# Moving work between the steps of a one-core hybrid decoder layer: gate steps, adaLN units, norm sums, attention steps and an early reload

## The chip, the cores and the metric

The kernel runs on one core of a Trainium2 chip, in float32 throughout. The metric is the device time of one execution in microseconds (us). The kernel before was timed three times: 1274.6, 1275.09 and 1276.74 us, median 1275.09.

## The reference

One decoder layer is run for a prompt of 512 tokens and for 8 sample tokens, with shared weights and D = 1024. `c` gives six adaLN vectors, which scale, shift and gate:

```python
shift1, scale1, gate1, shift2, scale2, gate2 = split(silu(c) @ w_ada + b_ada, 6)
h = modulate(rmsnorm(x, norm1_g), shift1, scale1)
gq, gk, gv, gr, glr, aq, ak, av, ga, gb = split(h @ w_in)
logg = log_sigmoid(glr @ gla_wg2 + gla_bg) / 16          # forget gates of branch A
y_a  = (rmsnorm(gla(gq, gk, gv, logg)) * silu(gr)) @ w_branch_a
# branch B: 3 groups of 8 heads, (window, dilation) = (128,1), (512,4), (2048,16);
# the groups' outputs are joined with weights from their softmax denominators
y_b  = o_att @ w_branch_b
x = x + gate1 * ((sigmoid(ga) * y_a + sigmoid(gb) * y_b) @ w_out)
h2 = modulate(rmsnorm(x, norm2_g), shift2, scale2)
a, b = split(h2 @ w_up)
x = x + gate2 * ((silu(causal_conv3(a)) * b) @ w_down)
y = rmsnorm(x, normf_g)
```

The samples attend to cached keys and values, and all the updated states and caches are outputs too.

## The kernel before

Activations lie feature-major: 8 tiles of 128 features by 520 tokens (512 of the prompt, 8 samples). Each weight matrix is streamed by SyncE in units of at most 1 MB into two slots `wraw`. Float32 precision is made out of three passes: ScalarE rounds a unit to `whi` (`split_hi`, L349), VectorE takes the rest as `wlo` (`split_lo`, L362), and TensorE multiplies hi by hi, hi by lo and lo by hi (`three_pass`, L378). A unit of two output tiles is 96 matmuls of 260 columns. This stream fills nearly the whole execution; everything else is pushed in between its matmuls.

How it is pushed in: the other work of a phase is written as generators (one each for TensorE, ScalarE and VectorE) that `yield` after each step. `Between` counts places in the stream (with `fine=True` eight places a unit, one after each 12 matmuls, without it four) and at each place advances the generator by as many steps as keep the steps spread evenly over the places. Where there are more steps than places, some places get two steps with no stream matmul between them. All three engines count alike, and semaphores order what they exchange. An engine executes its instructions strictly in the written order, so a step that waits stops the stream behind it.

The places and names that matter here:

- `gla_in_*`: the 28 steps beside the seven units of the phase `gla_in`. Steps 0 to 3 make the forget gates of the prompt: one matmul (L924), on ScalarE Abs, Exp and Ln (L887 to L889) with a load of another function table ahead of Exp and of Ln, and on VectorE one operation (L974). Step 4 does it for the samples, step 5 prepares the relative bias (L985), 6 to 9 are its matmuls (L939, L945).
- `heads_tok_*`, `attend_*`, `sample_*`, `join_*`: the steps of an attention phase. Values, keys and the new rows are turned to token-major, then come 8 or 16 score steps (scores L1543, exp L1678, turned probabilities L1555, times values L1568), then the cached keys of the samples. The last phase (`att2`) goes on with `join_*`: the joined output is turned (L1829) and split (`b2H`, `b2L`), then the samples' softmax (L1835, L1897 to L1910, L1841), their cached values (L1854) and their output (L1861, L1863). The stream of `att2` is the four units `gb`, whose tiles ScalarE copies (L433) and SyncE stores to a scratch tensor `raw_gates` (L446). The block of `att2` ends when SyncE has seen all these stores land (L1948).
- Each block ends in a barrier of all engines. The next block multiplies by w_branch_b (`bb`, two units of four tiles), w_branch_a (`ba`) and w_out (`wo`), four units of two tiles each. POOL reloads the raw gates `raw4` and the stored GLA output `oT4` (2 MB) at the start of this block; ScalarE takes sigmoids (L2020), VectorE multiplies (L2119, L2122), ScalarE rounds the product (L2067) and copies the `bb` tiles (L2078).
- adaLN: w_ada is cut in 24 units of 256 columns. A unit is 16 matmul records (L528), a copy (L547), a turn (L539) and an addition into `mod` (L552). Units 8 to 19 are interleaved with the stream; units 20 to 23 (all of them `gate2`, first read in the down projection) come in a row behind the last `wo` unit.
- Beside them runs the norm ahead of the FFN: squares on ScalarE (L602), their sum over the 8 tiles on VectorE (L611), a matmul with ones (`sums_pe`, L563), mean, root and Newton step (L570 to L597), a broadcast by matmul (L589). In the next block `modulate_ffn_*` makes `actH` and `actL` tile by tile, and the first FFN unit follows it tile by tile.

Of the kernel before, what the change touches and what calls it, by code (L numbers as in the profile page):

```python
# [5 lines left out]
F32 = mybir.dt.float32  # L6
# [5 lines left out]
P = 128  # L12
D = 1024
KD = D // P
TP = 512
# [20 lines left out]
N_HEAD, N_TAIL, N_ADA = 8, 20, 24  # L36
# [104 lines left out]
def program(nc, w, o, con):  # L141
# [23 lines left out]
    with ctx:  # L165
# [392 lines left out]
        def sums_pe(pe, i, bank, t):  # L558

            pe.wait_ge(s("sq_added"), (KD - 1) * i)  # L560
            for n in range(5):
                m = P if n < 4 else NS
                last = pe.matmul(ps[0:m, bank, n:n + 1], t[:, P * n:P * n + m], ones[:, 0:1], start=True, stop=True)  # L563
            last.then_inc(s("sq_summed"), 1)
# [34 lines left out]
        def square_act(act, i, k, X, tmp):  # L599
            if k >= 2:  # L600
                act.wait_ge(s("sq_added"), (KD - 1) * (i - 1) + max(1, k - 2))
            act.activation(tmp["sq"][:, k % 2, :], X[:, k, :], ACT.Square).then_inc(s("sq_ready"), 1)  # L602

        def square_dve(dve, i, k, tmp):
# [4 lines left out]
            if k >= 2:  # L609
                dve.wait_ge(s("sq_added"), (KD - 1) * (i - 1) + k - 1)  # L610
            dve.tensor_tensor(tmp["t"], tmp["sq"][:, 0, :] if k == 1 else tmp["t"], tmp["sq"][:, k % 2, :], ALU.add)\  # L611
               .then_inc(s("sq_added"), 1)

        def modulate_ffn_dve(dve, X, tmp):

            g = vec[:, V_N2:V_N2 + KD].unsqueeze(2).to_broadcast([P, KD, NC])
            shift, scale = 3 * KD, 4 * KD
            dch.link(dve, dve.scalar_tensor_tensor(tmp["A"], mod[:, scale:scale + KD, :], 1.0, g, ALU.add, ALU.mult))  # L618
            hs = tmp["hs"]
            dve.wait_ge(s("r_spread"), 2)  # L620
            dch.link(dve, dve.tensor_tensor(hs, X[:, :, TP:T], rS.unsqueeze(1).to_broadcast([P, KD, NS]), ALU.mult))
            dch.link(dve, dve.tensor_tensor(hs, hs, tmp["A"][:, :, 1:NC], ALU.mult))  # L622
            dve.tensor_tensor(hs, hs, mod[:, shift:shift + KD, 1:NC], ALU.add).then_inc(s("h_ready"), 1)

            def low(k):
                dve.wait_ge(s("h_hi"), KD + 2 + k)
                dve.scalar_tensor_tensor(actL[:, k, 0:TP], tmp["hf"][:, k % 2, 0:TP], mod[:, shift + k, 0:1],  # L627
                                         actH[:, k, 0:TP].bitcast(F32), ALU.add, ALU.subtract).then_inc(s("h_split"), 1)

            for k in range(KD):  # L630
# [4 lines left out]
                if k == 0:  # L635
                    dve.wait_ge(s("h_hi"), KD + 1)
                    dve.tensor_tensor(actL[:, :, TP:T], hs, actH[:, :, TP:T].bitcast(F32), ALU.subtract)
                else:
                    low(k - 1)
            low(KD - 1)  # L640

        def modulate_ffn_act(act, tmp):

            act.wait_ge(s("h_ready"), KD + 1)
            act.activation(actH[:, :, TP:T], tmp["hs"], ACT.Copy).then_inc(s("h_hi"), 1)
            for k in range(KD):
                act.wait_ge(s("h_normed"), KD + k + 1)
                act.activation(actH[:, k, 0:TP], tmp["hf"][:, k % 2, 0:TP], ACT.Identity, bias=mod[:, 3 * KD + k, 0:1])\
                   .then_inc(s("h_hi"), 1)

# [243 lines left out]
        V_LAG = 15  # L894
        IN_STEPS = 4 * len(GLA_IN)
# [20 lines left out]
        def gla_in_pe(pe):  # L916
            for p in range(IN_STEPS):
# [3 lines left out]
                if p < 4:  # L921
                    if p >= 2:
                        pe.wait_ge(s("g_ready"), p - 1)
                    pe.matmul(ps[:, 4 + p % 2, :], lrT[0:GR + 1, P * p:P * p + P], wg2, start=True, stop=True)\  # L924
                      .then_inc(s("z_ready"), 1)
                elif p == 4:
# [5 lines left out]
                elif 6 <= p < 6 + NG:  # L932
                    g = p - 6
# [7 lines left out]
                elif p == 6 + NG:  # L941
# [11 lines left out]
        def gla_in_act(act):  # L953
            for p in range(IN_STEPS):
                if p < 4:
                    act.wait_ge(s("z_ready"), p + 1)
                    if p >= 1:
                        act.wait_ge(s("g_ready"), p)
# [512 lines left out]
        def heads_tok_act(act, g):  # L1471
# [4 lines left out]
            for c in KOUT[g]:  # L1476
                yield
# [1090 lines left out]
```

## Time and profile before

| | |
|---|---|
| median of three runs | 1275.09 us |
| the profiled execution: time | 1278.76 us |
| its span, first to last instruction | 1277.1 us |
| TensorE matmul busy | 1204.9 us (94%) |
| VectorE, ScalarE, GpSimd busy | 623.9, 453.6, 107.2 us |
| mean granted TensorE clock | 0.968 of full |
| DMA | 229.41 MB, mean 180 GB/s |
| a weight split of 2048 columns, mean: ScalarE (L2260), VectorE (L2316) | 1.9, 2.3 us |
| a w_in load of 1 MB, issue to landing, median (38 issues) | 5.3 us |
| a w_ada load of 1 MB into `arena`, the same (12 issues) | 12.0 us |
| TensorE's waits for copies of turned probabilities (L1688) | 3.0 us in five, longest 1.1 |

TensorE is the busy engine. A busy time is not all useful time: where the granted clock is 0.50 (1.2 GHz in place of 2.4 GHz), a matmul is busy for longer. "Idle before" in a row is the time in which that engine did nothing ahead of that instruction, with the engine or transfer that ended the wait. The views used below are the waits (who waited for whom), windows (busy time and clock of given stretches), the timeline (instructions by time) and the chain of work that ended last.

### The profile page before, as it was taken

Reading aid. Unit: us, or ns where it says so; the run is one execution under the profiler, and the core shown is the slowest. Engines: PE = TensorE matmul, PEld = TensorE weight load, DVE = VectorE, ACT = ScalarE, POOL = GpSimd, SP = SyncE. Lnnn points to the kernel's source line nnn. Section 1 sums busy time; section 2 is a strip of 40 time slices with the busy share of each in tenths; the row PEclk is TensorE's granted clock in tenths of the full one; section 3 lists DMA queues with packets and bytes.
Section 4 is the critical chain, followed back from the end, with each engine's and each line's share of the span. In section 5 each row is a group of like instructions: output and inputs, shape, how many; then the busy total and the mean of one; then the engine's idle time right before and its main releaser. Section 6 shows DMA issues by size and latency. Waiting matters only on the chain. (4 is left out here: it accounts for less than half of the span.)

```text
span 1277.1 us, 23207 instructions
## 1 busy us (share of the span) xinstructions
PE 1204.9 (94%) x9743; PEld 1139.8 (89%) x9743; DVE 623.9 (49%) x1003; ACT 453.6 (36%) x652; POOL 107.2 (8%) x189
## 2 busy tenths in 40 slices
PE   5898999999989999999988989998999999999997
PEld 4777999988989999989887789987999999999997
DVE  3523224554534554266478175556666556643333
ACT  3273223544344441353243154224323332322222
POOL 0000002111011001110211111000000000000000
PEclk8898999999999999999988899997999999999999
DMA  9653539755345324333427477712878888256661
GB/s 303 182 186 118 170 117 346 274 181 169 104 149 163 100 64 161 114 104 104 130 71 260 151 247 280 235 34 67 264 256 279 285 265 258 83 176 222 222 224 67
DMA packets 166017, 229.41 MB, mean 180 GB/s; under 512 B 7644, under 2 KB 148342, under 8 KB 164636
## 3 DMA queue, kind: packets, MB, share of 16 engines
q1 hardware_dynamic: 148720, 123.72, 31.8%
q10 hardware_dynamic: 1684, 54.56, 11.7%
q0 software_dynamic: 15536, 50.01, 11.5%
q8 instruction: 59, 0.97, 0.3%
q14 instruction: 18, 0.15, 0.0%
HBM read 204.58 MB, written 81.87 MB: 224 GB/s over the span
## 5 line engine op out<-in xcount | busy, mean ns | idle before, releaser
L378 PE MATMUL ps<-actH,whi 128*128 128x260 f32 x2064 | 436.6, 293 | 10.7 <-DVE actL L627 4.0
L378 PE MATMUL ps<-actH,wlo 128*128 128x260 f32 x2064 | 419.9, 285 | 0.0
L378 PE MATMUL ps<-actL,whi 128*128 128x260 f32 x2064 | 419.2, 285 | 0.0
L378 PEld LDWEIGHTS ps<-actH,whi 128*128 128x128 f32 x2064 | 322.5, 192 | 29.9 <-issue 24.6
L378 PEld LDWEIGHTS ps<-actL,whi 128*128 128x128 f32 x2064 | 322.6, 191 | 0.0
L378 PEld LDWEIGHTS ps<-actH,wlo 128*128 128x128 f32 x2064 | 322.4, 191 | 0.0
L362 DVE TENSOR_TENSOR wlo<-wraw,whi 128x2048 fp32r<-128x2048 f32 (+2 forms) x95 | 141.2, 1498 | 155.1 <-ACT whi L349 154.8
L349 ACT ACTIVATE whi<-wraw 128x2048 fp32r<-128x2048 f32 (+2 forms) x95 | 119.4, 1274 | 122.4 <-PE ps L378 91.6
L433 ACT ACTIVATE arena<-ps 128x520 f32<-128x520 f32 x74 | 44.5, 601 | 221.3 <-PE ps L378 213.1
L378 PE MATMUL ps<-gH,whi 128*128 128x260 f32 x352 | 71.8, 285 | 0.0
L378 PE MATMUL ps<-gL,whi 128*128 128x260 f32 x352 | 71.3, 284 | 0.0
L378 PE MATMUL ps<-gH,wlo 128*128 128x260 f32 x352 | 71.2, 284 | 0.0
L2316 DVE TENSOR_TENSOR wlo<-wraw,whi 128x2048 fp32r<-128x2048 f32 x22 | 50.4, 2293 | 25.4 <-ACT whi L2260 25.4
L1678 ACT ACTIVATE arena<-arena 128x128 f32<-128x128 f32 (+1 forms) x96 | 34.1, 419 | 65.2 <-DVE arena L1651 65.1
L378 PEld LDWEIGHTS ps<-gL,whi 128*128 128x128 f32 x352 | 55.0, 190 | 0.0
L378 PEld LDWEIGHTS ps<-gH,whi 128*128 128x128 f32 x352 | 54.8, 190 | 0.1
L378 PEld LDWEIGHTS ps<-gH,wlo 128*128 128x128 f32 x352 | 54.7, 190 | 0.0
L2260 ACT ACTIVATE whi<-wraw 128x2048 fp32r<-128x2048 f32 x22 | 42.1, 1913 | 7.0 <-issue 7.0
L1646 DVE SCALAR_TENSOR_TENSOR arena<-ps,arena 128x512 f32<-128x512 f32 (+1 forms) x32 | 20.9, 654 | 35.9 <-PE ps L1543 35.2
L547 DVE COPY arena<-ps 128x256 f32<-128x256 f32 x24 | 10.1, 422 | 57.4 <-PE ps L528 57.4
L2242 POOL DMA_DIRECT2D out_conv_p<-arena x22 | 11.4, 518 | 316.6 <-DVE arena L2357 214.8
L2267 ACT ACTIVATE arena<-arena 128x520 f32<-128x520 f32 x22 | 14.1, 640 | 64.4 <-DVE arena L2333 64.4
(338 smaller groups left out, 1420.0 us busy)
## 6 DMA issues: line engine op xcount, KB each, us to landing
wraw<-in_w_in SPq DMA_DIRECT2D x38, 1024.0 KB, 5.3
out_win_s<-in_cache_win ACTq DMA_DIRECT2D x16, 2046.0 KB
wraw<-in_w_up SPq DMA_DIRECT2D x44, 512.0 KB, 5.8
out_win_s<-in_cache_win ACTq DMA_DIRECT2D x8, 2044.0 KB
arena<-in_w_ada SPq DMA_DIRECT2D x12, 1024.0 KB, 12.0
wraw<-in_w_ada SPq DMA_DIRECT2D x12, 1024.0 KB, 5.2
raw_gates<-arena SPq DMA_DIRECT2D x24, 260.0 KB, 6.2
arena<-raw_gates POOLq DMA_DIRECT2D x24, 260.0 KB, 4.3
```

The source lines that it names most:

```text
L349: ins = act.activation(whi[:, v % 2, c], wraw[:, u % 2, c], ACT.Copy)
L362: ins = dve.tensor_tensor(wlo[:, v % 2, c], wraw[:, u % 2, c], whi[:, v % 2, c].bitcast(F32), ALU.subtract)
L378: last = pe.matmul(ps[:, 2 * (n % 2) + a, 0:HT], wt, X[:, k0 + j, a * HT:a * HT + HT], start=begin and j == 0 and wt is hi and X is H, sto ...
L433: act.activation(halves(to), banks(n), ACT.Copy).then_inc(tile_read["act"], 1)
L547: dve.tensor_copy(rows[:, a % 2, :], ps[:, 7, 0:2 * P]).then_inc(ada_tok, 1)
L1646: dve.scalar_tensor_tensor(sv, ps[:, 4 + n % 2, 0:nh * J].rearrange("p (h k) -> p h k", k=J), SCALE, biasT[:, hs, lo:hi], ALU.mult, ALU.ad ...
L1678: last = act.activation(sv, sv, ACT.Exp, bias=own(g, c)[:, h:h + 1])
L2242: pool.dma_start(o["conv_p"][:, col], ast[0:2, store.slot, :]).then_inc(s(f"stored{store.slot}"), 16)
L2260: act.activation(whi[:, vn % 2, :], wraw[:, (up0 + 1 + d) % 2, :], ACT.Copy).then_inc(hi_ready, 1)
L2267: act.activation(sg5, acc, ACT.Sigmoid).then_inc(s("ffn_sig"), 1)
L2316: dve.tensor_tensor(wlo[:, vn % 2, :], wraw[:, (up0 + 1 + d) % 2, :], whi[:, vn % 2, :].bitcast(F32), ALU.subtract).then_inc(lo_ready, 1)
```

## The change

It edits the order of work and a few waits; almost no instruction is added or removed.

1. `gla_in`: the gate steps stand at every other step (0, 2, 4, 6), that of the samples at 8, the bias matmuls from 10 on; VectorE prepares the bias at step 7.
2. Last attention phase: the transposes of values and keys are taken in pairs, four steps in place of eight; one empty step ahead of the first score step and two behind it; the join gets two empty steps ahead of the turned softmax, the samples' cached values have six steps of their own, the output has one, and an empty step closes the phase: 39 steps in place of 36 over 32 places. In all attention phases the first scores wait for ScalarE's copies of the new rows only and no longer for VectorE's subtraction (L1503) behind them; the sample steps wait for that.
3. POOL issues the first four raw-gate loads and the load of `oT4` at the end of `att2`, not at the start of the next block. There the sigmoid of each `bb` unit's first tile stands ahead of the weight split.
4. N_TAIL goes from 20 to 22: units 20 and 21 are interleaved behind the third and fourth `ba` unit, and only 22 and 23 stand behind the last `wo` unit.
5. The ones matmul ahead of the FFN is in two parts, which add up in PSUM: the sum over seven tiles, and the eighth square by itself. VectorE's last addition goes. The FFN scale (L618) is computed ahead of the sums. Unit 23's turn is moved into the FFN block, and TensorE's root broadcast is behind the turn of unit 22.
6. `modulate_ffn_*`: the prompt's first tile comes ahead of the small operations on the samples.

```diff
-N_HEAD, N_TAIL, N_ADA = 8, 20, 24
+N_HEAD, N_TAIL, N_ADA = 8, 22, 24
...
-        def sums_pe(pe, i, bank, t):
-            pe.wait_ge(s("sq_added"), (KD - 1) * i)
+        def sums_pe(pe, bank, part, first):
             for n in range(5):
...
+                last = pe.matmul(ps[0:m, bank, n:n + 1], part[:, P * n:P * n + m], ones[:, 0:1], start=first and n == 0,
+                                 stop=not first and n == 4, skip_group_check=True)
+            return last
...
+            dve.wait_ge(s("r_spread"), 2)
+            normed(0)
+            dch.link(dve, dve.tensor_tensor(hs, X[:, :, TP:T], rS.unsqueeze(1).to_broadcast([P, KD, NS]), ALU.mult))
+            dch.link(dve, dve.tensor_tensor(hs, hs, tmp["A"][:, :, 1:NC], ALU.mult))
+            dve.tensor_tensor(hs, hs, mod[:, shift:shift + KD, 1:NC], ALU.add).then_inc(s("h_ready"), 1)
+            low(0)
...
+        Z_STEP, ZS_STEP, B_STEP = (0, 2, 4, 6), 8, 10
...
+        HSTEPS = (5, 8, 4)
+        GAPS = (0, 0, 1)
...
-            pe.wait_ge(s("new_tok"), token(g, 2))
+            pe.wait_ge(s("new_tok"), token(g, 1))
...
-        JOIN_STEPS = 4 + 2 + 1 + VSTEPS
+        JOIN_STEPS = 4 + 5 + VSTEPS + 2
...
                 for i in range(VSTEPS):
                     load_values(i)
+                pool.wait_ge(outs, n_outs[0])
+                pool.wait_ge(s("oj_T"), 4)
+                for r in range(4):
+                    slot_landed(pool, "vc", r, 16)
+                    load_raw(pool, r)
+                pool.wait_ge(s("spT"), 2)
+                pool.dma_start(oT4.rearrange("p k t -> p (k t)"), od).then_inc(s("o_back"), 16)
...
-                    split_hi(act, U[u]["i"] + 1)
                     for m in range(4):
                         q = 4 * j + m
                         sigmoid_act(act, q)
+                        if m == 0:
+                            split_hi(act, U[u]["i"] + 1)
...
                 ada_pe(pe, N_TAIL)
-                ada_turn_pe(pe, N_TAIL, ada4)
-                sums_pe(pe, 1, 5, n2["t"])
-                for a in range(N_TAIL + 1, N_ADA):
-                    ada_pe(pe, a)
-                    if a == N_TAIL + 2:
-                        spread_root_pe(pe, 1, tok2)
-                    ada_turn_pe(pe, a, ada4)
+                pe.wait_ge(s("sq_added"), KD - 2)
+                sums_pe(pe, 5, n2["t"], True)
+                pe.wait_ge(s("sq_ready"), KD)
+                sums_pe(pe, 5, n2["sq"][:, (KD - 1) % 2, :], False).then_inc(s("sq_summed"), 1)
+                ada_pe(pe, N_TAIL + 1)
+                ada_turn_pe(pe, N_TAIL, ada4)
+                spread_root_pe(pe, 1, tok2)
...
+                ada_turn_pe(pe, N_TAIL + 1, ada4)
                 first_unit()
```

What the change does to TensorE's order is seen at three places. First, the first scores of `att2` (L1543 before, L1586 now) and the turned probabilities (L1555, L1598); L378 is the stream. Before:

```order
L378 MATMUL ps<-actL,whi 128x260 x2
L378 MATMUL ps<-actH,wlo 128x260 x2
L1543 MATMUL ps<-arena 128x128 [waits s_read,new_tok]
L1543 MATMUL ps<-arena 128x128 x7
L1555 MATMUL ps<-cst,arena 128x128 [waits pT_ready,p_ready]
L1555 MATMUL ps<-cst,arena 128x128 x3
L378 MATMUL ps<-actH,whi 128x260 x2
```

and now:

```order
L378 MATMUL ps<-actL,whi 128x260 x2
L378 MATMUL ps<-actH,wlo 128x260 x2
L1586 MATMUL ps<-arena 128x128 [waits s_read,new_tok]
L1586 MATMUL ps<-arena 128x128 x7
L378 MATMUL ps<-actH,whi 128x260 x2
L378 MATMUL ps<-actL,whi 128x260 x2
L378 MATMUL ps<-actH,wlo 128x260 x2
```

The turned probabilities stood right behind the scores; now 36 stream matmuls (18 rows) are between them.

Second, the end of `att2`: the cached values (L1854 before), the samples' output (L1861 and L1863 before, L1916 and L1920 now) and the branch that ends the block (L1939, L2013). Before:

```order
L378 MATMUL ps<-actH,wlo 128x260 x2
L1854 MATMUL ps<-arena 32x512 [waits slot_in4]
L1854 MATMUL ps<-arena 32x512 x3
L1861 MATMUL ps<-cst,arena 128x8 [waits spT]
L1863 MATMUL ps<-arena 128x4 x2
L1861 MATMUL ps<-cst,arena 128x8
L1863 MATMUL ps<-arena 128x4 x2
L1861 MATMUL ps<-cst,arena 128x8
L1863 MATMUL ps<-arena 128x4 x2
L1861 MATMUL ps<-cst,arena 128x8
L1863 MATMUL ps<-arena 128x4 x2
L1939 UNCONDITIONAL_BRANCH
```

and now:

```order
L1916 MATMUL ps<-cst,arena 128x8 x3
L1920 MATMUL ps<-arena 128x4 [waits spT]
L1920 MATMUL ps<-arena 128x4 x3
L1920 MATMUL ps<-arena 128x4 [waits spT]
L1920 MATMUL ps<-arena 128x4 x3
L378 MATMUL ps<-actH,whi 128x260 x2
L378 MATMUL ps<-actL,whi 128x260 x2
L378 MATMUL ps<-actH,wlo 128x260 x2
L378 MATMUL ps<-actH,whi 128x260 x2
L378 MATMUL ps<-actL,whi 128x260 x2
L378 MATMUL ps<-actH,wlo 128x260 x2
L2013 UNCONDITIONAL_BRANCH
```

Before, the last stream matmuls stood ahead of the last four values and of the output; now 12 of them stand behind the output, and nothing is behind these.

Third, TensorE between the last `wo` unit and the FFN: adaLN units (L528), their turns (L539), the sums (L563 before, L562 now), the root broadcast (L589, L590). Before (the turn of unit 22, unit 23 and its turn follow the last row shown):

```order
L563 MATMUL ps<-cst,arena 128x1 [waits sq_added]
L563 MATMUL ps<-cst,arena 128x1 x3
L563 MATMUL ps<-cst,arena 8x1
L528 MATMUL ps<-arena,scP 32x256 [waits ada_tok,ada_tail_in]
L528 MATMUL ps<-arena,scP 32x256 x7
L539 MATMUL ps<-cst,arena 128x9 [waits ada_read,ada_tok]
L539 MATMUL ps<-cst,arena 128x9
L528 MATMUL ps<-arena,scP 32x256 [waits ada_tok,ada_tail_in]
L528 MATMUL ps<-arena,scP 32x256 x7
L589 MATMUL ps<-cst,arena 128x128 [waits r_ready]
L589 MATMUL ps<-cst,arena 128x128 x3
L590 MATMUL ps<-cst,arena 128x8
```

and now:

```order
L562 MATMUL ps<-cst,arena 8x1
L562 MATMUL ps<-cst,arena 128x1 [waits sq_ready]
L562 MATMUL ps<-cst,arena 128x1 x3
L562 MATMUL ps<-cst,arena 8x1
L528 MATMUL ps<-arena,scP 32x256 [waits ada_tok,ada_tail_in]
L528 MATMUL ps<-arena,scP 32x256 x7
L539 MATMUL ps<-cst,arena 128x9 [waits ada_read,ada_tok]
L539 MATMUL ps<-cst,arena 128x9
L589 MATMUL ps<-cst,arena 128x128 [waits r_ready]
L589 MATMUL ps<-cst,arena 128x128 x3
L590 MATMUL ps<-cst,arena 128x8
L2115 UNCONDITIONAL_BRANCH
```

Two adaLN units are gone from this place, a second set of sums is added, and the block ends right behind the broadcast.

## Rows read from the trace of the kernel before

**Rows 1.** Waits of TensorE, whole span: who was waited for: us, times, longest.
```profile
PE ps L1555 <- ACT arena L1678: 4.0, 2, 2.8
PE ps L378 <- ACT arena L2078: 4.0, 1, 4.0
...
PE ps L939 <- DVE arena L985: 3.3, 1, 3.3
PE ps L1841 <- DVE arena L1906: 3.1, 1, 3.1
...
PE ps L924 <- DVE arena L974: 2.1, 2, 1.1
...
PE ps L1543 <- DVE query_parts L1503: 1.7, 2, 1.5
...
PE ps L1835 <- DVE b2L L1891: 1.0, 1, 1.0
...
PE ps L378 <- PEq L1939: 0.9, 1, 0.9
PE ps L1861 <- DVE arena L1931: 0.9, 1, 0.9
```
**Rows 2.** Windows, TensorE: stretch, length, busy (instructions), granted clock, DMA share, GB/s.
```profile
100.20:107.00 6.80, 5.50 (x21) 0.50 0.49 154
639.50:646.20 6.70, 4.02 (x18) 0.50 0.84 256
694.10:700.80 6.70, 4.74 (x23) 0.50 0.21 81
718.00:728.10 10.10, 9.17 (x40) 0.50 0.36 110
738.50:741.70 3.20, 3.20 (x17) 0.50 0.56 133
858.00:878.30 20.30, 15.17 (x81) 0.50 0.19 53
```
**Rows 3.** Chain that ended last: start us, us, what; a unit at each clock.
```profile
872.38 14.40 PE ps L378 x96
...
1003.46 11.54 PE ps L378 x96
```
**Rows 4.** Timeline of ScalarE in gla_in: start us, us, instruction, idle before.
```profile
80.33 0.60 ACT L887 ACTIVATE arena<-ps 128x512 f32<-128x512 f32 x1 [0.33 <-DVE arena L974]
80.94 1.28 ACT L888 ACT_TABLE_LOAD   x1
...
85.63 0.60 ACT L887 ACTIVATE arena<-ps 128x512 f32<-128x512 f32 x1 [0.82 <-DVE arena L974]
```
**Rows 5.** SyncE's waits, 690 to 730 us.
```profile
SPq L1948 <- DMA raw_gates<-arena: 1.7, 1, 1.7
```
**Rows 6.** Timeline of ScalarE about the end of att2.
```profile
714.91 0.60 ACT L433 ACTIVATE arena<-ps 128x520 f32<-128x520 f32 x1 [9.91 <-PE ps L378]
```
**Rows 7.** Timeline of VectorE: the first product with the reloaded GLA output.
```profile
736.14 0.70 DVE L2122 TENSOR_TENSOR arena<-arena 128x520 f32<-128x520 f32 x1 [8.61 <-DMA arena<-gla_out]
```
**Rows 8.** Timeline of TensorE: an interleaved adaLN unit, then the end of wo.
```profile
755.35 1.07 PE L528 MATMUL ps<-wraw,scP 128*32 128x256 f32 x16
...
756.82 0.36 PE L378 MATMUL ps<-a2H,whi 128*128 128x260 f32 x1
...
852.91 1.07 PE L528 MATMUL ps<-arena,scP 128*32 128x256 f32 x16
...
855.90 1.15 PE L563 MATMUL ps<-cst,arena 128*128 128x1 f32 x9
...
861.35 2.08 PE L589 MATMUL ps<-cst,arena 128*128 128x128 f32 x8
```
**Rows 9.** Timeline of VectorE ahead of the first FFN unit.
```profile
868.90 0.06 DVE L2307 MEMSET arena<- 128x5 f32 x1 [0.35 <-PEq L2039]
...
869.30 0.22 DVE L621 TENSOR_TENSOR arena<-arena,ps 128x64 f32<-128x64 f32 x1
```

More of the change, by code:

```diff
@@ L1453, in heads_tok_pe @@
                 yield
-            for i, c in enumerate(KOUT[g]):
+            for i, c in enumerate(KOUT[g]) if g < NG - 1 else ():
                 if i >= 2:
@@ L1469, in heads_tok_pe @@
             yield
+            yield from pause(g, 1)
         def heads_tok_act(act, g):
@@ L1474, in heads_tok_act @@
                 act.activation(avt[:, c, :], ps[:, 4 + c % 2, :], ACT.Copy).then_inc(s("av_tok"), 1)
-                yield
-            for c in KOUT[g]:
+                if g < NG - 1 or c % 2:
+                    yield
+                if g == NG - 1 and c % 2:
+                    yield
+            for c in KOUT[g] if g < NG - 1 else ():
                 yield
@@ L1484, in heads_tok_act @@
             yield
+            yield from pause(g, 1)
         def heads_tok_dve(dve, g):
-            for c in range(4):
+            for c in range(4 if g < NG - 1 else 0):
                 yield
             for i in range(len(KOUT[g])):
+                if g == NG - 1 and i % 2 == 0:
+                    yield
                 n = K0[g] + i
@@ L1659, in attend_dve @@
                 yield
+                if j == 0:
+                    yield from pause(g, 2)
             settle(len(st))
@@ L1692, in attend_act @@
                 yield
+                if j == 0:
+                    yield from pause(g, 2)
             yield
@@ L1877, in join_act @@
             act.activation(SS, SS, ACT.Exp, bias=small[0:NR, 0:1], accum_out=small[0:NR, 1:2]).then_inc(s("sm_p"), 1)
-            for _ in range(2 + VSTEPS):
+            for _ in range(5 + VSTEPS):
                 yield
@@ L1937, in join_dve, with load_raw @@
             yield
+            yield
+        oT4 = at(0, KD, T)
+        ya, yb = at(12480, KD, T), at(16640, KD, T)
+        raw4 = at(20800, 4, T)
+        RAW = list(range(KD)) + [q + k * KD for q in range(KD) for k in (1, 2)]
+        def load_raw(pool, r):
+            q = RAW[r]
+            pool.dma_start(raw4[:, r % 4, :], rawd[:, T * q:T * q + T]).then_inc(slot_in("raw", r % 4), 16)
         with nc.Block() as block:
@@ L1995, in program @@
         G = {k: units(k) for k in ("bb", "ba", "wo", "up", "dn")}
-        RAW = list(range(KD)) + [q + k * KD for q in range(KD) for k in (1, 2)]
         def residual_dve(dve, n, q, gate):
```

199 lines of the change are left out of this document (112 added, 87 removed).

## The prediction

> **What bounds the kernel now.** I read the waits of TensorE first, then the granted clock in windows around each of them, then the timeline where an edit touches it. TensorE is busy for 94% of the span, and a unit of 96 stream matmuls takes 11.54 us at the upper clock [rows 3], so one place of 12 takes 1.44 us and one of 24 takes 2.9 us. The time is TensorE's: it moves only by what TensorE waits for, by the instructions it issues, and by the clock that it is granted. The reader is to see in [rows 1] that almost every wait ahead of the FFN is one that the change touches, and in [rows 2] that stretches at half the clock (1.2 GHz in place of 2.4) lie right behind such waits. A matmul there takes twice as long, so a low stretch costs half of its busy time. The FFN itself runs without gaps worth a term, and no edit reaches into it.
>
> **The sum is made against the profiled execution**, 1278.76 us (span 1277.1 and 1.7 around it). That is 3.7 above the median of the three runs, 1275.09; I take the same difference off the median.
>
> **Gate steps of gla_in.** One gate tile goes through ScalarE and VectorE in 5.3 us (85.63 less 80.33, [rows 4]), and ScalarE starts the next one only when VectorE is through. The steps stood one place of 2.9 us apart, so TensorE waited 2.1 us in two waits (L924), and 3.3 us for the bias (L939), which VectorE reached only behind the last gate [rows 1]. At every other place there are 5.8 us for 5.3, and more where an adaLN unit lies between; the bias is prepared at step 7 for a matmul at step 10. The steps also leave room on ScalarE for its two tile copies and one weight split per unit. Behind the 3.3 us wait the clock was at half over a stretch with 5.50 us busy [rows 2], 2.7 lost. The bounds are 5.4 (clock falls all the same) and 8.1; with the longest wait gone I take 8.1. **-8.1**
>
> A rule of the Trainium skill speaks against this. The row shows a table load of 1.28 us [rows 4], and the whole gate, with two of them, in 5.3. "ScalarE: Activation LUTs", section "What ACT_TABLE_LOAD costs", adds some 1.38 us of drain to a load, 2.7 us for each switch. If two drains had still to be added, an estimate by that page is 8.1 us a gate, over the 5.8, and TensorE would go on waiting; the trace does not agree, as 5.3 holds everything.
>
> **The first scores of all attention phases** waited for VectorE's subtraction, 1.7 us in two waits, the longer of 1.5 in the last phase [rows 1]. The other 0.2 goes, because the copies on ScalarE are done earlier. **-0.2**
>
> **Scores of the last phase.** Of the 1.5 us about 0.7 goes, one VectorE operation of such a width [rows 7], and 0.8 for ScalarE's three copies stays. The turned probabilities stood right behind the scores and waited 2.8 us for ScalarE's exponentials (the longer of the two under L1678, [rows 1]). Now three places, 4.3 us of stream, lie between: gone. The half clock behind it had 4.02 us busy [rows 2], 2.0 lost. The pairs of transposes ahead cost nothing: the instructions are the same, and each wait on a copy has at least one place in between. The key copy waits for the store of the buffer two copies earlier, and the pairs leave that store as much time as before. The short waits for copied probabilities further on (3.0 us in five over the whole span, by the table) stay, since those steps keep their distance. -0.7 -2.8 -2.0 = **-5.5** (bounds 3.5 and 6.3).
>
> **Join.** Before, 1.0 us for the last split and 3.1 us for the samples' softmax [rows 1]. The two empty steps put two places, 2.9 us, over the softmax: 0.2 remains. But the pair of joined tiles turned at one place shortens the cover of the splits, so the 1.0 stays, and VectorE now has a piece of the weight split ahead of the softmax and one behind it, on which the last unit's first matmul waits: I take 1.3 for both together. New waits 2.5 in place of 4.1: -1.6 (bounds 0 and -4.1). The half clock with 4.74 us busy goes, as no wait of 3 us is left: -2.4. **-4.0**
>
> **End of that phase.** The wait for the picked values, 0.9 (L1861), goes: 12 matmuls cover it. But the same step list now ends with stream matmuls. Before, the last values and the output stood behind the last stream tile, some 7 us in which ScalarE copied that tile (714.91, 0.60 long, [rows 6]) and SyncE stored it and saw it land 1.7 us after its issue [rows 5]; the gap at the block's end was 0.9 [rows 1]. Now nothing covers that: 0.7 for the copy and its start, about 2.0 for issue and landing, 0.5 for the barrier (the gap of 0.9 without the two small operations in it), 3.2 us. That is +2.3. The output's matmuls of 4 and 8 columns hardly load TensorE; before, the clock was at half from their middle on, up to 5.4 us into the next block (the fourth stretch of [rows 2]). I expect the same now, with the last 12 matmuls in it, 1.44 us more. -0.9 +2.3 +1.4 = **+2.8** (bounds -3.2 to +5).
>
> **Start of the bb units.** ScalarE could not copy the second tile before it had rounded a product that waited for `oT4`: VectorE was idle for 8.6 us until 736.14 [rows 7], and TensorE waited 4.0 us (L2078, [rows 1]). Issued from the step of the softmax on, some ten places earlier, it lands before the block begins; POOL has nothing else queued there, and what it waits for (old stores, the turned join, the weighted new values) lies behind it by then. Per tile ScalarE has three operations of 0.6 us [rows 6] in 2.9, and the split behind the first sigmoid still ends a tile early. The half clock behind the wait, 3.20 busy, goes too: 1.6. **-5.6** (bounds 4.0 and 5.6)
>
> **Between wo and the FFN.** The last stream matmul ends at 852.9, the first of the FFN starts at 872.38 [rows 3, 8]. In between now: unit 22, then the sum over seven tiles, which VectorE ends one addition and TensorE one turn earlier, at about 855.0 in place of 855.90 [rows 8]; two sets of sums for one, 2.3 us for 1.15, to 857.2, about where they ended before. The mean, root and Newton step run beside unit 23 (1.07) and a turn, to 859.4 with the lower clock setting in at 858. The broadcast, 2.6 us at that clock with its sample part (2.08 of it in the row), ends at 862.0 instead of 863.9, and the block ends there, without two units and three turns at half clock. VectorE starts the next block 0.6 us later, at 862.6 in place of 868.90 [rows 9]. From there to the first FFN matmul it took 3.5 us; the scale and three small operations, 0.22 us long [rows 9] and about 0.25 each with the step to the next, are no longer ahead: 2.5, so 865.1. That is -7.3. The first unit took 14.40 us in place of 11.54 because of the clock [rows 3]; I leave it so, and TensorE at half clock is slower than the tiles come. Units 20 and 21 reappear in the stream, each 1.47 us with its turn (756.82 less 755.35, [rows 8]) at the upper clock: +2.9. If the last weights arrive in time, no wait is added there. **-4.4** (bounds -2.5 and -7)
>
> **Sum:** -8.1 -0.2 -5.5 -4.0 +2.8 -5.6 -4.4 = -25.0. Profiled 1278.8 - 25.0 = 1253.8, and for the median 1275.1 - 25.0 = **1250.1 us**.
>
> **Rivals.**
> - *The waits go and the clock does not come back.* The four low stretches that I count as gone cost 2.7, 2.0, 2.4 and 1.6, 8.7 in all; if shorter waits close by keep them, -16.3 is left: 1258.8 us. For it: the clock also fell at 718 behind a wait of only 0.9 with matmuls of few columns. Against it: waits of 1.1 (L924, L1688) left it up.
> - *The clock stays up at the end of the last phase.* The 12 full matmuls behind the output could hold it: 1.4 is not paid and the half of 9.17 us [rows 2], 4.6, is gained: 1244.1. Against it stands the new idle of 3.2 us right behind them.
> - *A late weight load.* The load of the second wo unit has to wait until unit 21 is used, which is the start of the first wo unit. It has 11.5 us less the two splits of the table (1.9 and 2.3), 7.3 us. The table gives 5.3 us as median for a weight load, but 12.0 for loads that start among many; the tail loads start at the same time. With 12.0 TensorE waits 4.7: 1254.8.
> - *The gates still stall* (the change would not do what it says). If ScalarE is held up in each gate by two more operations of a table load's length [rows 4], 2.6 us, three steps lack 2.1 each, 6.3 in all: 1256.4. No row supports it. The page named above would make it so.
> - *Slower than before.* The last store, on which the block's end now hangs bare. It landed 2 us after issue when nothing else was in flight; now POOL puts four reloads and 2 MB into the DMA engines in that phase. The 2 MB took 12 us from the block's start to 736; a store held up as long costs 10, and 1260 results. It turns the sum over only if the store takes 25 us more, for which the rows have no example.
>
> **Chances.** Forecast 0.60, clock does not come back 0.13, clock stays up 0.13, late load 0.06, gates 0.03, held store up to 1270 0.02, slower than before 0.03. The forecast's own range is 1246 to 1254, from the bounds of the join (2.5), the block's end (2.5) and the tail (2). The range for 8 in 10 takes in most of the first two rivals: 1243.5 to 1259. A measurement of this kernel tells 0.2%, 2.6 us, from no change; all cases but the last two are faster by more. Faster 0.95, same 0.02, slower 0.03.
>
> **What would show it.** In the profile after: no wait above 0.5 us under the gate and bias matmuls and no 0.50 clock about 100 us; none between the first scores and the turned probabilities; the softmax wait under 1 us; a gap of about 3 us at the end of the last attention phase, ended by the landing of a store to raw_gates; none for the bb tiles; 12 us in place of 19.5 between the last wo and the first FFN matmul. I am wrong if a gap of 2 us or more stands anywhere else, if the low stretches stay in number, or if the gap at the block's end is as short as before.

## The result, and the profile after

| | before | changed kernel |
|---|---|---|
| time, median | 1274.84 us (1273.21 to 1276.74, 4 runs) | 1259.67 us (1257.51 to 1262.34, 4 runs) |
| ratio | | 0.9881, 95% interval 0.9858 to 0.9905 |
| profiled execution: time, span | 1278.76, 1277.1 us | 1262.34, 1260.7 us |
| mean granted clock | 0.968 | 0.973 |

The kernel is 15.2 us faster (12.1 to 18.1 by the interval). The forecast was 25.0 us, and its range ended at 1259.0, just below the median.

The waits of TensorE in the profile after (line waited at, who was waited for: us in all, times, longest) answer to [rows 1]:

```profile
PE ps L1885 <- DVE b2L L1950: 7.2, 1, 7.2
...
PE ps L378 <- PEq L2013: 3.4, 1, 3.4
...
PE ps L1586 <- ACT arena L1521: 0.7, 1, 0.7
...
PE ps L1879 <- DVE b2L L1950: 0.7, 1, 0.7
```

Three things are to be seen. The waits under the gates (L924, L939), under the softmax (L1841, now L1893) and at the second bb tile (L378 for ScalarE) have no row any more; of the two on the exponentials (L1555, now L1598) the one of 2.8 is gone. The gap at the block's end is 3.4 in place of 0.9, as forecast. And one long wait is new, the longest of the span: 7.2 us under the transposes of the joined tiles (`join_pe`), for VectorE's `b2L`. No term had it. Two small ones are new as well, 1.0 us ahead of the sums (L562) and 0.5 us ahead of unit 23's turn (L539), between wo and the FFN, where the forecast added none.

The windows (stretch, length, busy us of TensorE, weight load, VectorE, ScalarE and GpSimd, granted clock, DMA share, GB/s) of the low stretches answer to [rows 2]:

```profile
281.60:285.00 3.40, 3.40 (x20) 2.59 (x21) 0.00 (x0) 1.31 (x4) 2.04 (x3) 0.51 1.03 362
677.70:687.80 10.10, 5.12 (x23) 4.68 (x24) 6.19 (x14) 3.17 (x5) 0.00 (x0) 0.50 0.20 70
708.40:721.90 13.50, 10.14 (x47) 9.87 (x46) 3.89 (x4) 4.94 (x6) 0.54 (x1) 0.50 0.36 130
848.40:861.90 13.50, 11.44 (x58) 10.09 (x50) 9.35 (x25) 3.95 (x8) 0.00 (x0) 0.50 0.28 80
```

Those at 100, 639, 694 and 738 us are gone. The one at 677.7 is new, right behind the 7.2 us wait, and costs half of its 5.12 busy, 2.6 us. The one at 281.6 is new too (3.40 busy, up to 1.7 lost); it lies in the GLA phase, which no edit touches.

"Half of the busy time", in the prediction and here, is a little too much for the stream. TensorE's timeline where the clock comes back (start, us, instruction), pairs of stream matmuls at 0.50 and then at full clock:

```profile
717.35 0.64 PE L378 MATMUL ps<-b2H,whi 128*128 128x260 f32 x2
717.78 0.64 PE L378 MATMUL ps<-b2L,whi 128*128 128x260 f32 x2
...
722.05 0.40 PE L378 MATMUL ps<-b2H,wlo 128*128 128x260 f32 x2
722.29 0.40 PE L378 MATMUL ps<-b2H,whi 128*128 128x260 f32 x2
```

A pair follows the last by 0.43 us at half clock and by 0.24 at full, 1.8 times and not twice, so that a low stretch full of them costs 44% of its busy time.

Followed back, the 7.2 us lead through three engines. ScalarE's timeline (start, us, instruction, idle before and what ended it):

```profile
662.39 0.60 ACT L433 ACTIVATE arena<-ps 128x520 f32<-128x520 f32 x1 [3.26 <-PE ps L378]
...
669.08 2.00 ACT L1931 ACTIVATE b2H<-ps 128x512 fp32r<-128x512 f32 x2 [4.52 <-PE ps L1879]
670.85 0.66 ACT L349 ACTIVATE whi<-wraw 128x512 fp32r<-128x512 f32 x1
678.21 0.60 ACT L433 ACTIVATE arena<-ps 128x520 f32<-128x520 f32 x1 [6.70 <-DMA raw_gates<-arena]
678.71 1.96 ACT L1931 ACTIVATE b2H<-ps 128x512 fp32r<-128x512 f32 x2
```

TensorE waits for `b2L`, VectorE for `b2H` (L1931), and ScalarE's `b2H` stands behind its copy of the fifth gb tile (L433). That copy waited 6.70 us for a store: the spill buffer has two halves, and the store of the third gb tile still read this one. The queues of SyncE and of GpSimd show why (issue, us, operation):

```profile
662.67 0.38 SPq L335 DMA_DIRECT2D wraw<-in_w_branch_b  x1
663.10 0.98 SPq L446 DMA_DIRECT2D raw_gates<-arena  x2
```

```profile
653.92 3.03 POOL L2035 DMA_DIRECT2D arena<-in_cache_win  x4 [24.97 <-DVE arena L1691]
656.94 2.40 POOL L2038 DMA_DIRECT2D arena<-in_cache_win  x4
```

The second pair of rows is the loads of cached values. The third tile was copied at 647.65 (0.60 long), but its store was issued at 663.10 only: in `stream_sp` it stands behind the next weight load, which waits for a weight slot. By then the loads of cached values (5.1 MB: four of 1024 KB, four of 256 KB) had been under way for 9 us. DMA issues of 662.3 to 664.5 us (x, KB each, median us to landing):

```profile
wraw<-in_w_branch_b SPq DMA_DIRECT2D x1, 1024.0 KB, 14.9
raw_gates<-arena SPq DMA_DIRECT2D x2, 260.0 KB, 15.1
```

The same two rows before, where the store was issued at 668.45 and the value loads at 669.20, that is behind it:

```profile
wraw<-in_w_branch_b SPq DMA_DIRECT2D x1, 1024.0 KB, 5.6
raw_gates<-arena SPq DMA_DIRECT2D x1, 260.0 KB, 5.9
```

and the rows of SyncE, GpSimd and ScalarE before:

```profile
668.45 3.95 SPq L446 DMA_DIRECT2D raw_gates<-arena  x2
...
669.20 3.03 POOL L1961 DMA_DIRECT2D arena<-in_cache_win  x4 [27.35 <-DVE arena L1646]
...
671.45 0.60 ACT L433 ACTIVATE arena<-ps 128x520 f32<-128x520 f32 x1 [0.34 <-PE ps L378]
...
681.71 0.60 ACT L433 ACTIVATE arena<-ps 128x520 f32<-128x520 f32 x1 [5.81 <-PE ps L378]
```

The store landed at 674.4, and the copy into that half came at 681.71: 7 us to spare. The change ends the last scores earlier in the stream. The fourth gb tile was copied 2.3 us behind the first value load before (671.45, 669.20), and 8.5 us behind it after (662.39, 653.92).

### The profile page after: what moved, and what is told of

It reads as the page before. It is cut to its first block and busy times, and to the rows that moved or that the text cites. A ratio compares the mean times of both kernels' runs of the same rounds, so it can differ in the third digit from the quotient of the medians.

```text
span 1260.7 us, 23226 instructions
## 1 busy us (share of the span) xinstructions
PE 1200.1 (95%) x9753; PEld 1136.6 (90%) x9753; DVE 622.6 (49%) x1002; ACT 452.6 (36%) x652; POOL 107.6 (9%) x189
## 5 line engine op out<-in xcount | busy, mean ns | idle before, releaser
L378 PE MATMUL ps<-actH,whi 128*128 128x260 f32 x2064 | 435.9, 293 | 7.9 <-PEq L1833 2.2
L378 PE MATMUL ps<-actH,wlo 128*128 128x260 f32 x2064 | 419.1, 285 | 0.0
L378 PE MATMUL ps<-actL,whi 128*128 128x260 f32 x2064 | 418.4, 284 | 0.0
L378 PEld LDWEIGHTS ps<-actH,whi 128*128 128x128 f32 x2064 | 321.7, 191 | 27.5 <-issue 22.9
L378 PEld LDWEIGHTS ps<-actL,whi 128*128 128x128 f32 x2064 | 321.8, 191 | 0.0
L378 PEld LDWEIGHTS ps<-actH,wlo 128*128 128x128 f32 x2064 | 321.6, 191 | 0.0
L433 ACT ACTIVATE arena<-ps 128x520 f32<-128x520 f32 x74 | 44.5, 602 | 205.4 <-PE ps L378 198.6
L378 PE MATMUL ps<-gH,whi 128*128 128x260 f32 x352 | 71.8, 285 | 0.0
L378 PE MATMUL ps<-gL,whi 128*128 128x260 f32 x352 | 71.3, 284 | 0.0
L378 PE MATMUL ps<-gH,wlo 128*128 128x260 f32 x352 | 71.2, 284 | 0.0
L378 PEld LDWEIGHTS ps<-gL,whi 128*128 128x128 f32 x352 | 55.1, 190 | 0.0
L378 PEld LDWEIGHTS ps<-gH,whi 128*128 128x128 f32 x352 | 54.8, 190 | 0.0
L378 PEld LDWEIGHTS ps<-gH,wlo 128*128 128x128 f32 x352 | 54.7, 190 | 0.0
L2313 POOL DMA_DIRECT2D out_conv_p<-arena x22 | 11.5, 521 | 313.5 <-DVE arena L2429 210.6
L2079 DVE SCALAR_TENSOR_TENSOR arena<-ps,mod,arena 128x260 f32<-128x260 f32 x16 | 7.8, 488 | 53.4 <-PE ps L378 53.4
```

What stands on the lines that cost most here:

```text
L378: last = pe.matmul(ps[:, 2 * (n % 2) + a, 0:HT], wt, X[:, k0 + j, a * HT:a * HT + HT], start=begin and j == 0 and wt is hi and X is H, sto ...
L433: act.activation(halves(to), banks(n), ACT.Copy).then_inc(tile_read["act"], 1)
L2079: dve.scalar_tensor_tensor(xT[:, q, 0:HT], a, g, xT[:, q, 0:HT], ALU.mult, ALU.add)
L2313: pool.dma_start(o["conv_p"][:, col], ast[0:2, store.slot, :]).then_inc(s(f"stored{store.slot}"), 16)
```

## The experiments

The loads of cached values are 5.1 MB where the expectations say 6, and they start at 653.92 where these say 652.5; against the copy of the third gb tile they moved closer by 8.5 us (14.8 behind it before, 6.3 after), not by 4. Each kernel was timed in five rounds beside the kernel before; ratios are to that, microseconds are the ratio's distance from 1 times 1275. "Held store" is the theory of the last paragraphs.

**The changed kernel again, for comparison.**

> The changed kernel itself on the chip of these runs, so that they can be set against it: the ratio to the kernel before as measured already, 0.986 to 0.991, that is 1257 to 1263 us. Every theory expects the same.

Measured: 1260.92 us, ratio 0.9884 (0.9858 to 0.9909), and the 7.1 us wait again. The result repeats.

**The store issued first.**

```diff
-def store_spilled(sp, u):
+def store_spilled(sp, u, tiles=(0, 1)):
...
-    for m in range(x["mt"]):
+    for m in tiles:
...
 for u in us:
-    issue(sp, u + 3)
-    store_spilled(sp, u)
+    early = (0,) if U[u].get("phase") == "att2" else ()
+    store_spilled(sp, u, early)
+    issue(sp, u + 3)
+    store_spilled(sp, u, tuple(m for m in (0, 1) if m not in early))
```

> The changed kernel, with one difference: in the last attention phase SyncE issues the store of a unit's first gb tile ahead of the next weight load, not behind it. Theory (held store): the store of the third gb tile was ready at 648.3 but stood in SyncE's order behind a weight load until 663.1, by when 6 MB of cached values filled the DMA engines, so it landed at about 678 and held ScalarE's copy, ScalarE's b2H behind it, VectorE's b2L and TensorE's transposes (7.2 us). Issued at 648.4 it lands before the value loads start at 652.5: the wait of 6.7 on ScalarE, the 7.2 on TensorE and the half clock at 677.7 (5.1 busy, 2.6 lost) go; 1 to 2 come back as the short waits that they had covered. The median falls by 7 to 10 us against the changed kernel, to about 1251. Rival (the pair of transposes itself makes TensorE wait for VectorE, whatever ScalarE does): the wait at the third transpose stays above 3 us and the time changes by less than 3 us. Rival (the value loads delay every store): a later store, of the fourth or fifth tile, holds its copy instead, 3 us or more on ScalarE, and the gain is under 4 us.

Measured: 1252.51 us, ratio 0.9826 (0.9802 to 0.9850), 8.4 us less than the changed kernel beside it. The landing of the third tile's store, by the issues of 649 us, and TensorE's waits of 630 to 730 us:

```profile
raw_gates<-arena SPq DMA_DIRECT2D x1, 260.0 KB, 2.0
```

```profile
PE ps L378 <- PEq L2015: 3.4, 1, 3.4
...
PE ps L378 <- DVE wlo L362: 1.2, 1, 1.2
PE ps L1887 <- DVE b2L L1952: 1.0, 1, 1.0
PE ps L1881 <- DVE b2L L1952: 0.7, 1, 0.7
```

The 7.2 is 1.0, ScalarE waits for no DMA, and the window where the clock was low has full clock and 8.87 us busy in place of 5.12:

```profile
677.70:687.80 10.10, 8.87 (x71) 7.44 (x71) 8.47 (x19) 3.39 (x7) 0.53 (x1) 1.00 0.66 209
```

The rival that blames the pair of transposes falls, and so does the one by which another store holds its copy. But early issue, idle DMA engines and a free buffer all come together here; the next two take them apart.

**The value loads later.**

```diff
 pool.wait_ge(s("s_read"), J0[g_last] + len(steps(g_last)))
+r = spill_order.index((us[1], 0))
+pool.wait_ge(s(f"spill_out{r % 2}"), 16 * (r // 2 + 1))
```

> The changed kernel, with one difference: GpSimd issues the six loads of cached values only when the store of the third gb tile has landed, so SyncE's order is left as it is and the store meets idle DMA engines. Theory (the store is late by the loads that fill the DMA engines, not by its late issue alone): issued at about 663.1 it lands at 665 to 666, ahead of the copy at 671.5, and the 7.2 us wait goes here too. The value loads start at 666 in place of 652.5, and take 25 to 32 us; the matmuls that read them start at about 690, so 0 to 5 us of wait for a slot may show there. The median falls by 3 to 9 us against the changed kernel. Rival (the late issue alone is enough): the wait of ScalarE on the store stays above 3 us and nothing is gained.

Measured: 1252.33 us, ratio 0.9822 (0.9799 to 0.9844), 8.6 less than the changed kernel. The store was issued as late as ever in the stream (660.73), 0.43 us behind the 1024 KB weight load, and took 6.1 us. The rival, that late issue alone holds the copy, falls: it needs the loads ahead as well. I had feared up to 5 us of TensorE waiting for values; there was none. ScalarE did wait 19.4 us for a later store (until 699.90), at a place where TensorE needed nothing from it: the waits of TensorE are those of the run before.

**A third buffer.**

```diff
+SPILL_SLOT = [r % 2 for r in range(16)] + [1, 2, 0, 1, 2, 0, 1, 2]
...
+def spill_buf(r):
+    return at(11648, T) if SPILL_SLOT[r] == 2 else spill[:, SPILL_SLOT[r], :]
...
-to = spill[:, r % 2, :]
+to = spill_buf(r)
```

> The changed kernel, with one difference: the gb tiles go through three buffers in the last attention phase in place of two; SyncE's order and GpSimd's value loads are left as they are. Theory (ScalarE waits only because the store of two tiles earlier still reads its buffer): the store issued at about 663 lands as late as before, near 678, but the copy at 671.5 has another buffer, whose store is long over, so the waits of 6.7 on ScalarE and 7.2 on TensorE go without any transfer being earlier. 6 to 9 us less than the changed kernel, about 1252.5, as with the store issued first. Rival (what helped in the two runs before was less traffic at 663 to 678, not the free buffer; ScalarE or VectorE is slowed by the transfers themselves): the wait at the third joined tile stays above 3 us.

Measured: 1251.67 us, ratio 0.9815 (0.9795 to 0.9835). Here the store is as late as in the changed kernel (first fence), and ScalarE does not care (second):

```profile
wraw<-in_w_branch_b SPq DMA_DIRECT2D x1, 1024.0 KB, 14.6
raw_gates<-arena SPq DMA_DIRECT2D x2, 260.0 KB, 14.8
```

```profile
670.91 0.64 ACT L440 ACTIVATE arena<-ps 128x520 f32<-128x520 f32 x1
```

This is the cleanest of the three: 14.8 us to landing and no wait. The price was that of a buffer not free in time, not of traffic that slows the engines.

**The join's steps as before.**

```diff
-JOIN_STEPS = 4 + 5 + VSTEPS + 2
+JOIN_STEPS = 4 + 2 + 1 + VSTEPS
```

and with it `join_pe`, `join_act` and `join_dve` of the kernel before.

> The changed kernel with the join of the last attention phase (positions of its steps for softmax, values and output) as in the kernel before; the pairs of head transposes, the pause and all the rest stay changed. Theory (held store): the wait at the third joined tile stays, 5 to 8 us, since it comes from ScalarE's held copy and not from the join's steps; the softmax wait (3.1 before) is back at 1 to 3 us, the gap at the block's end is near 1 in place of 3.4. In all within 3 us of the changed kernel. Rival (the new positions of the join's steps make the wait): the 7.2 us wait goes and the time falls by 5 us or more against the changed kernel.

Measured: 1261.66 us, ratio 0.9885 (0.9859 to 0.9911): level with the changed kernel. ScalarE waited 11.5 us for the store. TensorE's waits in 640 to 724 us, first rows and the softmax:

```profile
PE ps L1879 <- DVE b2L L1941: 4.2, 1, 4.2
...
PE ps L1891 <- DVE arena L1956: 1.5, 1, 1.5
```

The rival falls: without the join's new positions the hold is there, a place earlier and spread over more waits (4.2 where I expected 5 to 8 at the third tile). The gap at the block's end was 0.9 again, as expected. What is left is the earlier end of the scores, which starts the value loads earlier; that the early loads are needed is shown by the run with the value loads later, but no run takes the new score steps (pairs and empty steps) away by themselves.

**Each part alone, on the kernel before.** The edits are the parts of the change itself: gates; tail (22 for `N_TAIL`, the sums, the FFN scale, the order in `modulate_ffn_*`); reload; attention steps with join.

> The kernel before with one part of the change alone: the gates of gla_in in every other step. Theory (the forecast's term): the waits under the gate and bias matmuls (2.1 and 3.3 us) and the half clock about 100 us go, 8.1 us less than before. Rival (the clock falls again a little later, as it did about 282 us in the changed kernel): a new low stretch of 3.4 us, or more of them, takes 1.5 to 3 us back, and 5 to 6.5 us are gained.

> The kernel before with one part of the change alone: two adaLN units moved into the stream, the sums of squares in two parts, the later order of the adaLN scale. Theory (the forecast's term): 4.4 us less than before, with a longer time before wo's last tile (+2.9) and 7.3 less behind it. Rival (a late weight load for the second wo unit, 4.7 us of wait): no gain, within 1 us of before; the changed kernel's trace showed no such wait, so I give it little.

> The kernel before with one part of the change alone: the GLA output and the first four raw tiles loaded in the attention phase, the weight split of the bb units behind the first sigmoid. Theory (the forecast's term): the wait of 4.0 us at the second bb tile and the half clock behind it go, 5.6 us less than before (4.0 to 5.6). Rival (its loads hold up the last store at the block's end, or its waits on GpSimd come late): the gap at the block's end grows from 0.9 by 2 us or more and under 3.5 us are gained.

> The kernel before with one part of the change alone: the steps of the last attention phase and of the join. The forecast's terms for it were -0.2 -5.5 -4.0 +2.8 = -6.9 us. Theory (held store, as the changed kernel's trace and the run with the store issued first show): the wait of 7 us at the third joined tile comes with this part, by itself and without the other three, since the value loads now start 4 us closer behind the third gb tile's store; the join and the block's end cost 5 to 6 in place of the forecast's -1.2, and the part as a whole gives nothing: within 2.5 us of before. Rival (the held store needs the other parts too, by the loads of the early reload): no wait on a store above 2 us, and 6 to 9 us gained.

| part alone | forecast, us | ratio (95% interval) | us |
|---|---|---|---|
| gates | -8.1 | 0.9933 (0.9908 to 0.9958) | -8.5 |
| tail | -4.4 | 0.9970 (0.9949 to 0.9991) | -3.8 |
| reload | -5.6 | 0.9955 (0.9936 to 0.9973) | -5.7 |
| attention steps and join | -6.9 | 1.0001 (0.9982 to 1.0021) | +0.1 |

Three terms stand, each within its interval; the fourth gave nothing. The sum is -17.9, against -15.2 for all together; the 2.7 between them is less than the intervals can tell, and nothing here explains it. The fourth kernel's longest wait is the changed kernel's:

```profile
PE ps L1874 <- DVE b2L L1939: 7.3, 1, 7.3
```

So the hold comes with this part by itself, without the loads of the early reload. With the gates alone the clock is at half from 280.2 for 3.4 us; with the tail, the reload or the attention steps alone it is not. The rival for the gates is therefore seen in the trace, but the interval of -5.4 to -11.7 can't tell a gain of 8.1 from one of 6.4.

**Attention steps and join, with the store first,** on the kernel before.

> The kernel before with the steps of the last attention phase and of the join, and the store of a gb tile issued ahead of the weight load. It was 0 with the steps alone. Theory (the forecast's terms for this part were right but for the held store): -0.2 -5.5 -4.0 +2.8 = -6.9 us against before, 1266 to 1269, with a join that waits 2.9 us in all (0.7, 1.0, 1.2, as when the store was issued first in the changed kernel) and a gap of 3.4 at the block's end. Rival (something else in the new steps costs several us too): under 4 us gained.

Measured: 1268.99 us, ratio 0.9944 (0.9924 to 0.9964): -7.1 us against a forecast of -6.9, with join waits of 0.7, 0.9 and 1.2. The rival (under 4 us) falls. The interval reaches from -4.6 to -9.7.

**The block's end without the last store, store first, third buffer.**

```diff
-for d in range(3):
+for d in range(2):
     spill_landed(sp, d, len(spill_order))
...
+if r == 4:
+    spill_landed(pool, 2, len(spill_order))
...
+if j == 1:
+    spill_landed(dve, 2, len(spill_order))
```

The first is SyncE's wait at the block's end, the others stand in the next block, ahead of GpSimd's first load and in VectorE's first tile of the second bb unit.

> The changed kernel with the store issued first, the third buffer, and the block's end no longer waiting for the last store (it lies in the third buffer; GpSimd waits for it ahead of its loads in the next block, VectorE ahead of its first write over that buffer). Theory: the gap of 3.35 at the end of the last attention phase falls to 1.2 to 1.8 us (0.7 for ScalarE's last copy, 0.5 for the barrier), 1.7 to 2.1 less; with the store issued first that is about 1250.5 us. The low stretches about 700 to 712 may shorten, up to 2 more. Rival (the barrier waits for something else, SyncE's issue or VectorE's piece of a weight split): the gap stays above 2.8 us.

Measured: 1251.80 us, ratio 0.9814 (0.9794 to 0.9835). The gap did what was expected:

```profile
PE ps L385 <- PEq L2022: 1.7, 1, 1.7
```

The time didn't follow: it is level with the third buffer alone (1251.67) and with the store first. Part of it is the clock. The low stretch at the block's end, of this kernel and then of the one with the third buffer alone:

```profile
700.60:710.60 10.00, 8.30 (x38) 8.03 (x39) 2.52 (x4) 4.52 (x5) 0.54 (x1) 0.50 0.30 107
```

```profile
702.70:712.70 10.00, 6.62 (x31) 6.35 (x30) 3.69 (x3) 4.65 (x5) 0.54 (x1) 0.50 0.31 105
```

It is as long, but TensorE is busy for 8.30 us of it in place of 6.62, so some 0.8 of the 1.7 us is paid back at half clock. What is left is below what the runs can tell.

> The changed kernel with the store issued first once more, on the chip of these runs, to set the other three against it: a ratio to the kernel before of 0.980 to 0.985, as before.

Measured: 1252.14 us, ratio 0.9824 (0.9801 to 0.9847). The three repairs and their combination can't be told apart; all four beat both kernels, by about 22 to 24 us against before.

## Why the prediction was right in part

| step of the prediction | forecast | trace after | |
|---|---|---|---|
| gates | -8.1 | -7.7 by the end of gla_in | right |
| (none) low clock at 281.6 | 0 | +1.3 | missed |
| first scores | -0.2 | about -0.5 | right |
| last phase: scores, join, block's end | -6.7 | 0.0 | wrong |
| start of the bb units | -5.6 | -5.5 | right |
| between wo and the FFN | -4.4 | -3.9 | right |

Each entry is the shift of the same instruction against before, less the shift at the entry above. In the first, 0.4 us is against the gates: this execution reached the phase so much later (68.29 us, 67.89 before), so the phase itself gave 8.1. The entries add up to -16.3, and the two spans differ by 16.4; the medians differ by 15.2. The fourth runs from the last phase's first stream matmul to the first bb matmul. These are the two ends after:

```profile
610.11 0.48 PE L378 MATMUL ps<-actH,whi 128*128 128x260 f32 x2 [1.10 <-PEq L1833]
...
715.91 0.77 PE L378 MATMUL ps<-b2H,whi 128*128 128x260 f32 x2 [3.36 <-PEq L2013]
```

That is 105.80 us. Before it was 105.83:

```profile
616.97 0.47 PE L378 MATMUL ps<-actH,whi 128*128 128x260 f32 x2 [1.10 <-PEq L1783]
...
722.80 0.77 PE L378 MATMUL ps<-b2H,whi 128*128 128x260 f32 x2 [0.93 <-PEq L1939]
```

With the store issued first it is 98.27 (611.01 to 709.28), 7.6 less, where the forecast was 6.7. The half clock at the block's end cost less than forecast: half of 10.14 busy, 5.1, where 4.6 and 1.4 make 6.0. The fifth and sixth have their ends in

```profile
730.29 1.07 PE L528 MATMUL ps<-wraw,scP 128*32 128x256 f32 x16
...
856.12 0.77 PE L378 MATMUL ps<-actH,whi 128*128 128x260 f32 x2 [1.59 <-DVE actL L641]
```

against 742.66 and 872.38 [rows 3].

**The step that failed** is the join, "-4.0": "New waits 2.5 in place of 4.1", and the half clock "goes, as no wait of 3 us is left". Its own reasoning held: with the hold away the new waits are 0.7, 1.0 and 1.2, 2.9 in all, and no low stretch lies there. What it left out is a DMA that moved. I had moved the scores earlier in the stream and priced TensorE's transposes ("cost nothing: the instructions are the same"), but their last score releases 5.1 MB of loads on GpSimd. They changed places with a store on SyncE, whose landing frees a buffer that ScalarE copies into. The chain from there to TensorE has four links, all visible before: the in-order queue of SyncE, the two halves of `spill`, ScalarE's copy ahead of `b2H`, VectorE's `b2L`. Cost: 7.2 of wait less the 1.0 that stays, plus 2.6 of half clock (2.3 at 44%), less 1.2 of a wait for `wlo` that it covered: 7.6 us. The traces differ by 7.5 there (105.80 less 98.27), the ratios 0.9884 and 0.9826 by 7.4.

**The rival was at the wrong place.** I did name a held store, at the block's end, with 10 us as its price and 0.02 as its chance. SyncE's wait for the landing there was 1.7 us, as before; the same mechanism struck 38 us earlier (678.2, where the next block starts at 715.9), where the store is not waited for by the block but by a copy. I had looked at stores only where a row showed a wait for one. Before, the copy had 7 us to spare, so no row showed it.

**The gates.** The prediction held a table rule against this term: "ScalarE: Activation LUTs", section "What ACT_TABLE_LOAD costs", in the Trainium skill adds a drain to each load, by which TensorE would have gone on waiting. By that rule this trace disagrees: no wait under the gates is left in it, and the gate matmuls stand 7.0 us apart (71.38 and 78.39) where a gate of 8.1 us would have left one. The 5.8 us of the prediction are the stream alone, without the gate's own matmuls (1.12 us).

**The rest of the distance.** The repaired kernels are at 0.9814 to 0.9826, the forecast is at 0.9804, 1 to 3 us less. The low stretch at 281.6 has 1.3 of it. It follows a wait of 2.5 us that stood there before as well, without a low stretch. It was in eight of the nine profiles with the gates moved (not with the value loads later), and in none of the five without. Why it comes with them is open.

**The clock's rival** ("the waits go and the clock does not come back", 1258.8) came close to the time by another way: three of the four low stretches counted as gone stayed away (100, 639, 738), and the one in the join came back behind the new wait only.

## What to carry to other kernels

When steps are moved, list for each semaphore in them which DMA it releases, on any queue, and look at what else is in flight then; a reordering that leaves every engine's work the same can still change places between a 5 MB load and a small store. For every buffer with two halves, work out the spare time between landing and reuse from issue and landing, though no wait is shown: 7 us to spare were gone with one edit. And a store behind a load in one in-order queue is issued when the load may be, not when its data is ready.

## What the runs showed of the hardware

A store of 260 KB landed 2.0 us after its issue when nothing else was in flight (the store issued first). It took 5.9 us before and 6.1 us with the value loads later, both times 0.43 us behind a 1024 KB load on the same queue. It took 15.1 us in the changed kernel, behind the same load and with GpSimd's 5.1 MB begun 9 us ahead of it. Before, these loads were issued too, 0.75 us behind the store, and it landed as soon as without them. So the weight load ahead makes some 4 us, and the head start of the value loads the other 9. The windows of the changed kernel (columns as above) from the store's issue to its landing:

```profile
662.00:666.00 4.00, 4.00 (x27) 3.24 (x27) 3.86 (x7) 2.16 (x4) 0.00 (x0) 1.00 1.02 384
666.00:670.00 4.00, 4.00 (x32) 3.62 (x32) 2.19 (x4) 0.92 (x2) 0.00 (x0) 1.00 1.05 294
670.00:674.00 4.00, 3.33 (x30) 3.16 (x29) 2.64 (x3) 1.51 (x3) 0.00 (x0) 1.00 1.04 240
674.00:678.00 4.00, 1.46 (x13) 1.25 (x11) 0.00 (x0) 0.00 (x0) 2.18 (x4) 0.95 1.09 338
```

They moved 5.0 MB in 16 us, of which 1.6 MB (1024 and twice 260 KB) were SyncE's, just under a third. The view of the DMA queues shows how that share came about. From 663.1 to 666.0 us all 288 packets were of GpSimd's queue (q0) and none of SyncE's (q1); why, no view shows. From 667 to 673 us (packets, MB, share of the engines' time):

```profile
q0 software_dynamic: 276, 0.92, 63.6%
q1 hardware_dynamic: 279, 0.57, 41.1%
```

The queues moved as many packets each, but GpSimd's held 3.3 KB on average and SyncE's 2.0 KB, so SyncE got 38% of the bytes. The Trainium skill, "DMA: Bandwidth & Descriptors", section "Queues, rings and completion order", says that a DMA engine takes a packet from each queue row in turn. By that rule the trace agrees in this stretch, if the packets of the view are those of the page.

The granted clock differs between executions of one program: the kernel with the store first had 13.7 us at half clock from 839.0 in one profile (span 1251.5) and 3.4 us from 845.2 in the other (span 1247.9), with the same waits in the join and the same gap at the block's end. These two ran on different chips, but it holds on one as well: in six executions of the changed kernel on one chip the mean granted clock went from 0.973 to 0.980 and the span from 1261.4 to 1255.6 us. A difference of 2 or 3 us between two profiled spans of this kernel need not be the edit's.
